# Order of loads in the first DMA queue, and order of GpSimd's work at the turn of the delta-rule loop, in a fused two-layer kernel

## The reference

```python
mod = silu(c) @ mod_w + mod_b                  # mod_w is 2048 x 12288
sh1, sc1, ga1, sh2, sc2, ga2 = split(mod, 6)
h = x * (1 + sc1) + sh1
qkv, z, b, a = split(h @ gdn_w_in)             # 2048 x 12352
qkv = silu(causal_depthwise_conv(qkv, conv_w)) # 4 taps
q, k = l2norm(q) / sqrt(128), l2norm(k)        # 16 heads of 128
v                                              # 32 heads of 128
beta = sigmoid(b);  g = -exp(a_log) * softplus(a + dt_bias)
o = gated_delta_rule(q, k, v, g, beta)         # per head, triangular solve, state 128 x 128
o = rmsnorm(o) * norm_w * silu(z)
x = layer_norm(alpha * x + (1 + ga1) * (o @ gdn_w_out))
...                                            # SwiGLU, then the second layer (conv + S5 scan hybrid)
```

## Time and profile before

| | |
|---|---|
| median of three runs | 3103.24 us |
| the profiled execution | 3100.09 us |
| its span, first to last instruction | 3098.5 us |
| mean granted TensorE clock | 0.964 |
| TensorE busy | 93% |
| VectorE busy | 62% |
| ScalarE busy | 39% |
| GpSimd busy | 28% |
| DMA | 178 GB/s over the span |

### The profile page before, as it was taken

The page is one execution under the profiler, slowest core; times in us unless marked ns, Lnnn a source line. Parts: engine busy times, 40 slices in busy tenths (PEclk is TensorE's granted clock), DMA queues, the critical chain, the costliest instruction groups (busy, mean ns, idle before and its releaser), DMA issues.

```text
span 3098.5 us, 54050 instructions
## 1 busy us (share of the span) xinstructions
PE 2885.7 (93%) x21277; PEld 2713.9 (88%) x21277; DVE 1927.0 (62%) x2399; ACT 1218.9 (39%) x1496; POOL 872.0 (28%) x584
## 2 busy tenths in 40 slices
PE   2559999999999899999999999979999999999998
PEld 2558999999999888899999999968988889999996
DVE  5446465465465465766665666676688888654454
ACT  1114435534534534444333333434333333433343
POOL 2326556555566573000000000000444544000000
PEclk7769999999999999999999999999999999999999
DMA  7645565565565455666666666644544545555554
GB/s 248 222 172 184 164 197 184 165 203 174 168 202 178 163 184 183 194 200 184 185 187 187 186 184 187 185 149 143 154 154 140 161 142 158 163 188 182 188 198 149
DMA packets 285852, 552.90 MB, mean 178 GB/s; under 512 B 18881, under 2 KB 56306, under 8 KB 284530
## 3 DMA queue, kind: packets, MB, share of 16 engines
q1 hardware_dynamic: 266482, 474.81, 49.6%
q0 software_dynamic: 19200, 75.54, 6.4%
HBM read 548.19 MB, written 2.10 MB: 178 GB/s over the span
## 4 chain that ended last, share of the span: by engine, by line
PE 61%; issue 14%; POOL 11%; DVE 9%; DMA 2%; ACT 1%; SPq 1%; POOLq 0%; DVEq 0%; ACTq 0%
PE pg L989 32%; PE pd L1002 10%; POOL wl L576 8%; PE pd L989 6%; PE pg L1002 3%; PE pg L769 3%; DVE arena L1591 2%; PE pg L788 2%; DMA arena<-in_mod_w 1%; POOL arena L570 1%; DVE wl L1813 1%; PE pd L1130 1%; PE pd L716 1%; PE pd L744 1%; PE pd L1119 1%
## 5 line engine op out<-in xcount | busy, mean ns | idle before, releaser
L1813 DVE TENSOR_TENSOR wl<-wr,wh 128x1024 fp32r<-128x1024 f32 x616 | 765.0, 1252 | 568.9 <-ACT wh L1379 567.6
L1379 ACT ACTIVATE wh<-wr 128x1024 fp32r<-128x1024 f32 x616 | 652.2, 1059 | 1050.1 <-PE pg L989 702.5
L989 PE MATMUL pg<-hh,wh 128*128 128x256 f32 x2944 | 838.0, 285 | 8.5 <-issue 4.5
L989 PE MATMUL pg<-hl,wh 128*128 128x256 f32 x2944 | 831.2, 282 | 0.0
L989 PE MATMUL pg<-hh,wl 128*128 128x256 f32 x2944 | 830.7, 282 | 0.0
L576 POOL TENSOR_TENSOR wl<-wr,wh 128x1024 fp32r<-128x1024 f32 x216 | 532.2, 2466 | 534.2 <-ACT wh L1208 533.6
L989 PEld LDWEIGHTS pg<-hh,wh 128*128 128x128 f32 x2944 | 562.0, 191 | 33.4 <-issue 26.4
L989 PEld LDWEIGHTS pg<-hl,wh 128*128 128x128 f32 x2944 | 562.2, 191 | 0.5
L989 PEld LDWEIGHTS pg<-hh,wl 128*128 128x128 f32 x2944 | 562.3, 191 | 0.0
L1208 ACT ACTIVATE wh<-wr 128x1024 fp32r<-128x1024 f32 x216 | 228.0, 1057 | 543.9 <-PE pg L769 463.1
L769 PE MATMUL pg<-hh,wh 128*128 128x256 f32 x1472 | 431.0, 293 | 1.1 <-ACT arena L1252 1.1
(11 more groups left out here) (357 smaller groups left out, 4584.0 us busy)
## 6 DMA issues: line engine op xcount, KB each, us to landing
wr<-in_w_in SPq DMA_DIRECT2D x224, 512.0 KB, 3.9
wr<-in_ffn_w_gu SPq DMA_DIRECT2D x176, 512.0 KB, 4.4
wr<-in_gdn_w_in SPq DMA_DIRECT2D x128, 512.0 KB, 4.2
arena<-in_mod_w POOLq DMA_DIRECT2D x64, 1024.0 KB, 6.8
wr<-in_ffn_w_down SPq DMA_DIRECT2D x88, 512.0 KB, 4.5
arena<-in_mod_w SPq DMA_DIRECT2D x32, 1024.0 KB, 9.6
wr<-in_gdn_w_in SPq DMA_DIRECT2D x128, 256.0 KB, 2.9
wr<-in_gdn_w_out SPq DMA_DIRECT2D x56, 512.0 KB, 4.3
```

Of the source, the lines that this page charges most:

```text
L989: m = nc.tensor.matmul(bank[:, n * T:(n + 1) * T], w[s][:, k, n * P:(n + 1) * P], act[x][:, k0 + k, :], skip_group_check=True, start=(firs ...
L1379: a(wh[c % 4][:], wraw[c % 4], ACT.Copy).then_inc(s_hc, 1)
L1813: v.tensor_tensor(wl[c % 4][:], wraw[c % 4], wh[c % 4][:].bitcast(F32), ALU.subtract).then_inc(s_lc, 1)
```

## The change

Four edits. In the SP queue, chunks 4 and 5 go behind mod 8 and mod 9, chunks 6 to 11 go one each behind mod 16 to 21, chunks 12 to 17 behind mod 24 to 29, chunks 18 to 23 behind mod 31. In GpSimd's `batch`, the order is rowm, sqb, (in the last round `o_low(1)`), and then the two loads. `sqb` waits for the SiLU of q and k alone, by a semaphore of its own, and ScalarE no longer waits on itself between the two SiLU. In the last round `o_high(1)` is done in the turn, and `o_high` and `o_low` come one piece earlier and at the head of a step; GpSimd's pieces and VectorE's get separate semaphores.

```diff
-GO = order("sq", "rowm")
+GO = order("rowm", "sq")
...
             for t in range(4, 32):
                 mod_load(t)
-                c, i = t // 8, t % 8
-                if t == 7:
-                    gdn_load(0, 4)
-                    gdn_load(0, 5)
-                if c in (1, 2) and i in (3, 7):
-                    for n in range(3):
-                        gdn_load(0, 6 * c + 3 * (i // 4) + n)
-                if t == 27:
-                    gdn_load(0, 18)
-                    gdn_load(0, 19)
-            for n in range(20, NCH):
+                if t in (8, 9):
+                    gdn_load(0, t - 4)
+                if t >= 16 and t % 8 < 6:
+                    gdn_load(0, 6 * (t // 8) - 6 + t % 8)
+            for n in range(18, NCH):
                 gdn_load(0, n)
...
                 restart()
-                for t in range(2):
-                    mod_load(it * 8 + 32, t)
-                pool.wait_ge(s_a, it * len(AO) + 1)
-                nc.gpsimd.tensor_tensor(sqb, qk.rearrange("p a b -> p (a b)"), qk.rearrange("p a b -> p (a b)"),
-                                        ALU.mult).then_inc(s_g, 1)
                 rows = gcT[0:NH].rearrange("p (c t) -> p c t", c=TT).unsqueeze(2).broadcast_to([NH, TT, VH, P])
                 pick = ident[0:NH, bass.ds(it * VH, VH)].unsqueeze(1).unsqueeze(3).broadcast_to([NH, TT, VH, P])
                 nc.gpsimd.tensor_tensor(rowm[0:NH], rows, pick, ALU.mult).then_inc(s_g, 1)
+                pool.wait_ge(s_qk, it + 1)
+                nc.gpsimd.tensor_tensor(sqb, qk.rearrange("p a b -> p (a b)"), qk.rearrange("p a b -> p (a b)"),
+                                        ALU.mult).then_inc(s_g, 1)
+                if o_low:
+                    o_low(1)
+                for t in range(2):
+                    mod_load(it * 8 + 32, t)
                 for t in range(1, 22):
+                    if o_low and t < 6:
+                        o_low(t + 1)
                     low(it + 1, t + 2)
-                    if o_low and t < 7:
-                        o_low(t)
...
-                if c < 12:
-                    pe.wait_ge(s_os, kp // 2 + 1)
+                if c == 0:
+                    pe.wait_ge(s_osv, 1)
+                elif 2 <= c < 12:
+                    pe.wait_ge(s_os, kp // 2)
...
-                link(a(qk.rearrange("p a b -> p (a b)"), pend[:, 0:4, :].rearrange("p a b -> p (a b)"), ACT.Silu))
+                a(qk.rearrange("p a b -> p (a b)"), pend[:, 0:4, :].rearrange("p a b -> p (a b)"), ACT.Silu).then_inc(s_qk, 1)
...
                 for t in range(1, 24):
+                    if t < 6 and not taps:
+                        o_high(t + 1)
...
-                    if t < 7 and not taps:
-                        o_high(t)
...
-            turn(NIT - 2, lambda: o_high(0))
+            turn(NIT - 2, lambda: (o_high(0), o_high(1)))
```

More of the change, by code:

```diff
@@ L329, in build @@
         s_cd = sem("s_cd")
+        s_qk = sem("s_qk")
         s_zo = sem("s_zo")
@@ L362, in build @@
         s_os = sem("s_os")
+        s_osv = sem("s_osv")
         s_hm = sem("s_hm")
@@ L1032, in _ @@
                 if t < 8:
-                    pe.wait_ge(s_os, k // 2 + 1)
+                    pe.wait_ge(s_os, 6)
+                    if k >= 14:
+                        pe.wait_ge(s_osv, 2)
                 elif t == 8:
@@ L1829, in _ @@
             v.tensor_tensor(fl(o_s[1][:, 0:4, :]), fl(oT[:, 0:4, :]), fl(o_s[0][:, 0:4, :]).bitcast(F32),
-                            ALU.subtract).then_inc(s_os, 1)
+                            ALU.subtract).then_inc(s_osv, 1)
             steps = delta(NIT - 1, False)
```

## The result

The changed kernel takes 3072.45 us (median of four, 3069.46 to 3077.64) against 3103.44 us: a ratio of 0.990, 95% interval 0.988 to 0.992. I had forecast 3056 and a range of 3042 to 3070. The direction was right, a third of the gain is missing, and the time lies above the range. The profiled execution took 3073.22 us with a span of 3071.6, so 26.9 us less than the one before, where the medians differ by 31.0.

A forecast was written before the change was run, and what follows sets the result against it. Early TensorE waits for VectorE's sums, held by `mod_w` loads stuck in the SP queue; in the rounds TensorE is the bound. 3103.24 - 36.4 - 5.2 - 0.5 + 1.8 - 7 = 3056 us, range 3042 to 3070.

The forecast's parts named there:

- Edit 1, the queue: New SP load order at the start: idle pieces -36.4 us, sums at full clock -5.2 us.
- The three idle pieces: TensorE's idle before the sums of groups 3, 5, 7 goes whole: 12.82 + 12.83 + 10.74 = -36.4 us.
- the three sums: Sums of groups 3, 5, 7 at full clock; 1.84 us against 3.58 in parts 1 and 2: -5.2 us, bound 0.
- the chain just added up: Loads, VectorE's groups and h in the first half, named as late next; slack put at 14 to 15 us.
- Edit 2, the turn: GpSimd's order at six turns: `sqb` 0.35 us later, TensorE's wait 2.54 to 2.9 us, +1.8 us; round 0 -0.5 us.
- the rival that the loads' issue hid a larger price: At the turns, `sqb` comes free after all: up to 15 us more gain, 3041 us; chance 0.04.
- Edit 3, the last round: Pieces of o made earlier in the last round: -7 us, bounds -4 and -9.
- The 6.63 us: TensorE's last-round wait at ochunk 2 for GpSimd's first low piece of o, forecast to go.
- the 7.4: In the last round the Gram products start at 1085.5 instead of 1092.96: -7.4 us.
- The clock: TensorE's clock draw at the turns taken as equal, 0; bounds -12.6 and +15.6 us.
- Loads that are slower than VectorE: At the start, bigger loads lie on VectorE's path: 24 us come back, 3080 us; chance 0.05.
- The clock at the turns: Rival: TensorE's clock falls long at all turns, +15.6 us, 3072 us; chance 0.05.

The follow-up runs named there:

- squares_first: The changed kernel with GpSimd's squares (`sqb`) before the gate rows (`rowm`), both before the two loads; 3051.61 us, ratio 0.983 to the kernel before.
- gap: The changed kernel with GpSimd's low parts of chunks 8 and 9 in the last round made to wait for VectorE steps; 3070.38 us, ratio 0.989.
- late_mods: The changed kernel with VectorE's last-round multiply-adds for mod, all but step 0's, two steps later; 3068.98 us, ratio 0.989.
- best_gap: squares_first with 1 + scale straight from PSUM, the early pieces of o and GpSimd's last-round pause; 3047.01 us, ratio 0.982.

## Why the prediction was wrong

**Edit 1, the queue: right in the main.** The three idle pieces went whole, and the three sums ran at 1.84 us, to the hundredth. Of the -41.6 us, the traces show -37.8 at the gate sums of part 3 (220.85 to 183.07). The missing 3.8 us are in the main the 3.9 by which TensorE's waits behind its sums grew with VectorE's small operation. The forecast named "the chain just added up" as what is late next, and costed that chain by its rows with GpSimd quiet. Moving h forward by 12.8 us moved it beside GpSimd's low part. So a cost of 3.9 us stood in the sum at nothing. From the gate sums to the first sums of round 0 it takes 35.06 us instead of 33.70, where 0.5 less was forecast. At the transposes before chunk 22 (200 to 205 us) the granted clock is 0.70; in the same place before (238 to 243 us) it was 1.00.

**Edit 2, the turn: right.** The wait is 2.86 us a turn where 2.9 was forecast, and the rival that the loads' issue hid a larger price is out. squares_first shows what the order could have given: the edit put the wrong one of the two operations first. What the Trainium skill, SBUF, State Buffer (section "SBUF: two separate sides") states of the two engines, weighed there, did not make TensorE wait longer at the turn: `rowm` started on time, and it was VectorE's copies that took long beside it, in squares_first up to 3.16 us:

```profile
447.36 3.16 DVE L1657 COPY arena<-vc 128x8 f32 x1
```

**Edit 3, the last round: wrong, and the step that failed.** I wrote -7 us with bounds -4 and -9, and that GpSimd "is two pieces ahead, but I count some 0.4 us for a low part that is late". It measured +4.5 us, which is 11.5 of the 20.4 us by which the two spans miss the forecast. The 6.63 us did go, and the Gram products did start earlier: 16.0 us behind the first sums of round 7 (1054.37 - 1038.39), where it had been 21.9 (1092.96 - 1071.05). So 5.9 us of the 7.4 were there. Then GpSimd, with all its inputs ready, ran without a gap, one multiply-add of VectorE was held for 12.37 us, and TensorE waited 5.75 us for the mask behind it. I had looked at GpSimd's time for its own work, and not at what it does to VectorE while it works. gap and late_mods show this from both sides: pause GpSimd, or take the multiply-adds out of the way, and the round is 117 to 118 us. Even so it is only 1 to 2 us shorter than before, so -7 was too much in any case. In gap the Gram products start 15.8 us behind the first sums of round 7, so 6 us earlier than before, but TensorE's waits in the round still sum to 7.5 us against 9.4: in place of 6.63 at ochunk 2 there are 2.71 for ScalarE's copy of v and 1.13 and 0.65 for GpSimd's low parts. Which of them is the price of the early pieces no run takes apart.

**The clock.** The forecast took the clock as it was before, apart from the sums of groups 3, 5 and 7. Between the first sums of rounds 0 and 7 the change lost 3.8 us, of which 1.9 are the six longer waits and 0.9 the longer wait at ochunk 0 (4.95 instead of 4.01, where VectorE's low part of o took 3.2 us beside GpSimd's `rowm`); about 1 is left for the clock (TensorE's busy time between the marks is 798.3 us against 797.3). That explains little of the miss, but the clock limits what a single version can tell: late_mods and gap gained 5 to 6 us in the round they aim at, lost 3 to the clock in the round before it, and show 2 to 3.5 in the median.

**The rivals.** Loads that are slower than VectorE: no, it never waits for `mod_w` over 0.3 us in groups 3 to 7. The clock at the turns, for which the Trainium skill, TensorE: Matmul & The Clock Gate ("HAM oscillation") says that idle gaps bring the lower clock back: the traces agree in part. In squares_first waits of 0.95 to 2.25 us left the sums at 1.98 us in six turns of seven, and in the change waits of 2.78 to 4.10 us did so in one of seven. But 1.83 us was followed by sums of 3.29 in squares_first, and the same wait of 2.25 us in round 0 by 1.98 in squares_first and by 3.50 in best_gap, so the length of the wait alone does not decide. The rival I did not have was the one that happened: GpSimd, with its inputs ready earlier, holds up VectorE.

## What to carry to other kernels

Before pulling GpSimd's work forward, list what VectorE does in that stretch from SBUF to SBUF, and in what order: work of low priority ahead of the critical operation can be held and then holds it, as the mask here. Gaps between GpSimd's operations, placed where VectorE has critical work, took the long operation from 13.92 to 6.98 us in gap. In a queue of loads, a load that waits for the consumer's progress belongs behind all loads that do not, and this alone was worth 36 us here; when two operations feed the next engine, put first the one that it waits for first.

## What the runs showed of the hardware

VectorE operations from SBUF to SBUF and GpSimd's wait for each other here, and for whole operations. A 128x4 operation took 1.6 to 1.8 us and ended 0.02 us after GpSimd's; with an input in PSUM it took 0.16 us. The Trainium skill, SBUF, State Buffer (section "SBUF: two separate sides") states this for VectorE operations in a two-port mode or with two inputs in SBUF, and calls the shared pair "an exclusive lock, not a bandwidth split"; the rows agree with the lock. What I had not expected is that the loser can lose several times running: one multiply-add was held across five operations, although its record starts at 1067.63 and that of the first of them at 1067.78 (starts on GpSimd are rough). Before, GpSimd's operations followed each other too and the two took turns: VectorE's pairs took 4.3 us, and GpSimd's low parts up to 2.8. In the change GpSimd kept its 2.3 to 2.4 us for five operations, and VectorE's pair took 13.92 (1.52 and 12.37). What decides between the two patterns is open; no run here tells it.
